# The end of the output projection in a streaming-encoder layer: another order, and four subtractions on GpSimd

## The reference, cut to what matters

```python
mix = jnp.concatenate([y_a, y_b], -1) @ w_out
x = layer_norm(ALPHA * x + (1 + g1) * mix, ln1_g, ln1_b)
h = layer_norm(x) * (1 + sc2) + sh2
gate, up = jnp.split(h @ w_ffn_up, 2, axis=-1)      # D_FF = 2816, so 22 column blocks of 128 each
ffn = (jax.nn.silu(gate) * up) @ w_ffn_down
x = layer_norm(ALPHA * x + (1 + g2) * ffn, ln2_g, ln2_b)
```

## Time and profile before

| what | value |
|---|---|
| three runs | 1384.96, 1387.47, 1394.6 us; median 1387.47 |
| the profiled execution | 1386.77 us; its span, first to last instruction, 1384.7 us |
| mean granted TensorE clock | 0.987 of full speed |
| PE, DVE, ACT, POOL busy | 96%, 68%, 42%, 40% of the span |
| output projection | about 547 to 661 us of the span |
| first pair of column blocks | about 662 to 693 us |

### The profile page before, as it was taken

The page is one execution under the profiler, slowest core; times in us unless marked ns, Lnnn a source line. Parts: engine busy times, 40 slices in busy tenths (PEclk is TensorE's granted clock), DMA queues, the critical chain, the costliest instruction groups (busy, mean ns, idle before and its releaser), DMA issues.

```text
span 1384.7 us, 28725 instructions
## 1 busy us (share of the span) xinstructions
PE 1331.2 (96%) x10596; PEld 1212.7 (88%) x10596; DVE 946.9 (68%) x1477; ACT 578.1 (42%) x1278; POOL 550.5 (40%) x622
## 2 busy tenths in 40 slices
PE   6999899989999999999899999999999999999997
PEld 4799899988977888887899999999999997887675
DVE  6526786865368877787796766556666558676388
ACT  6523343346476766244633333333333326443120
POOL 4887868682033334132234234434234331000041
PEclk9899999999999999999999999999999999999999
DMA  9422344345356653522314543545534459995894
GB/s 343 134 83 70 107 110 116 108 113 148 95 171 203 200 192 139 163 91 77 92 48 154 193 136 126 181 138 185 187 130 134 162 182 388 372 312 213 286 324 172
DMA packets 184404, 234.60 MB, mean 169 GB/s; under 512 B 17708, under 2 KB 118640, under 8 KB 184304
## 3 DMA queue, kind: packets, MB, share of 16 engines
q1 hardware_dynamic: 180128, 221.36, 49.1%
q10 hardware_dynamic: 4176, 11.89, 2.2%
HBM read 170.29 MB, written 61.73 MB: 168 GB/s over the span
## 4 chain that ended last, share of the span: by engine, by line
PE 56%; DVE 10%; issue 3%; ACT 3%; DMA 2%; POOL 1%; POOLq 0%; ACTq 0%; SPq 0%; DVEq 0%
PE bank L2533 30%; PE bank L2447 11%; PE bank L308 3%; PE bank L1803 2%; PE bank L2464 1%; PE bank L1840 1%; ACT hp L1909 1%; PE bank L1180 1%; DVE Lc L1632 1%; PE bank L1195 1%; DVE stat L1942 1%; DVE xt L1979 1%; DVE split L2576 1%; PE bank L1237 1%; PE bank L1226 1%
## 5 line engine op out<-in xcount | busy, mean ns | idle before, releaser
L2447 PE MATMUL bank<-split 128*128 128x512 f32 x924 | 212.4, 390 | 3.7 <-DVE split L2580 3.3
L2447 PEld LDWEIGHTS bank<-split 128*128 128x128 f32 x924 | 172.7, 188 | 45.5 <-DVE split L2576 6.8
L2533 PE MATMUL bank<-Tlo,rh 128*128 128x272 f32 x640 | 184.7, 289 | 0.0
L2533 PE MATMUL bank<-Thi,rh 128*128 128x272 f32 x640 | 184.2, 288 | 0.0
L2533 PE MATMUL bank<-Thi,rl 128*128 128x272 f32 x640 | 184.0, 288 | 0.0
L308 PE MATMUL bank<-hT_hi,whi 128*128 128x384 f32 (+1 forms) x504 | 167.8, 333 | 3.8 <-DVE wlo L298 3.6
L308 PE MATMUL bank<-hT_lo,whi 128*128 128x384 f32 (+1 forms) x504 | 165.8, 329 | 0.0
L308 PE MATMUL bank<-hT_hi,wlo 128*128 128x384 f32 (+1 forms) x504 | 165.7, 329 | 0.0
L2533 PE MATMUL bank<-hT_lo,rh 128*128 128x272 f32 x480 | 138.5, 289 | 0.0
L2533 PE MATMUL bank<-hT_hi,rl 128*128 128x272 f32 x480 | 138.4, 288 | 0.0
L2533 PE MATMUL bank<-hT_hi,rh 128*128 128x272 f32 x480 | 137.9, 287 | 0.0
(11 more groups left out here) (463 smaller groups left out, 3246.7 us busy)
## 6 DMA issues: line engine op xcount, KB each, us to landing
wada<-w_ada SPq DMA_DIRECT2D x12, 2048.0 KB, 11.0
raw<-w_up SPq DMA_DIRECT2D x40, 512.0 KB, 5.1
wsum<-w_down SPq DMA_DIRECT2D x11, 1024.0 KB, 5.6
wt<-wsum SPq DMA_DIRECT2D x11, 1024.0 KB, 4.0
rW<-wt SPq DMA_DIRECT2D x44, 256.0 KB, 6.4
split<-split SPq DMA_DIRECT2D x22, 512.0 KB, 4.9
wraw<-w_in SPq DMA_DIRECT2D x21, 512.0 KB, 4.1
rows<-convrow ACTq DMA_DIRECT2D x16, 577.5 KB, 3.7
```

What stands on the lines that cost most here:

```text
L2447: last = pe.matmul(ps[down_bank(q, r)][:], a[:, rows], w, start=(k == 0 and m == 0), stop=(k == KH - 1 and m == 2))
L2533: last = pe.matmul(ps[banks[c]][:, 0:NC], w[:, ks], a, start=(n < 3 and k == 0 and p == 0), stop=(k == 3 and p == 2), skip_group_check=True)
```

## The change

Nothing is computed differently; instructions change their engine or their place in a queue, all in steps 6 to 8.

- `ffn_lo(0, 0)` and `ffn_lo(0, 1)` (the low parts of the weights) and `split_h2(5)` and `split_h2(6)` go from VectorE to GpSimd, into steps 6 and 7, two in each.
- ScalarE's `ffn_hi(0, 0)` goes from step 7 to step 6, `modulate(5)` from step 7 to step 6, ahead of norm(6); `modulate(6)` from step 8 to step 7, ahead of norm(7); `modulate(7)` from before norm(8) to behind it.
- TensorE makes (0, 0) chunk 1 before `transposes(7)`, not after.

The diff, without the lines of `ffn_lo` for the second pair, which only wait for one more count that is always reached:

```diff
-        def ffn_lo(dve, i, j):
+        def ffn_lo(eng, i, j):
             if i == 0:
-                split_lo(dve, slot_of(j), R_FF + j + 1)
+                slot = slot_of(j)
+                eng.wait_ge(on["w_hi"], count(R_FF + j + 1))
+                eng.tensor_tensor(wlo[:, slot, :], wraw[:, slot, :], whi[:, slot, :].bitcast(F32), ALU.subtract).then_inc(on["w_lo"], 1)
                 return
...
             ffn_block(pe, 0, 0, (0,))
+            ffn_block(pe, 0, 0, (1,))
             transposes(PTILES - 1, (PTILES - 1) % 2)
-            ffn_block(pe, 0, 0, (1,))
             ffn_block(pe, 0, 1, (0,))
             transposes(PTILES, PTILES % 2)
...
# ScalarE, step(t, s)
-                if not (isinstance(t, int) and t < 2):
+                if not (isinstance(t, int) and (t < 2 or t > PTILES - 2)):
                     modulate(t - 2)
+                if isinstance(t, int) and t == PTILES - 2:
+                    act.wait_ge(on["wo_mm"], since("wo_mm", PTILES))
+                    ffn_hi(act, 0, 0)
+                    modulate(PTILES - 3)
                 if isinstance(t, int) and t == PTILES - 1:
-                    for j in range(2):
-                        act.wait_ge(on["wo_mm"], since("wo_mm", PTILES + j))
-                        ffn_hi(act, 0, j)
-                if isinstance(t, int) and t == PTILES:
-                    modulate(PTILES - 1)
+                    act.wait_ge(on["wo_mm"], since("wo_mm", TILES))
+                    ffn_hi(act, 0, 1)
+                    modulate(PTILES - 2)
...
             wo_steps(act, step)
+            modulate(PTILES - 1)
             modulate(PTILES)
...
# VectorE, step(t, s)
-                if isinstance(t, int) and t == PTILES:
-                    ffn_lo(dve, 0, 1)
...
-                if not (isinstance(t, int) and t < 2):
-                    split_h2(t - 2)
+                if not (isinstance(t, int) and (t < 2 or t > PTILES - 2)):
+                    split_h2(dve, t - 2)
...
-                if isinstance(t, int) and t == PTILES - 1:
-                    ffn_lo(dve, 0, 0)
...
# GpSimd, step(t, s)
                 pool.tensor_tensor(rstd[0:n, 0, 0:1], rstd[0:n, 0, 0:1], mhalf[0:n, 0:1], ALU.pow).then_inc(on["o_rs"], 1)
+                if isinstance(t, int) and t in (PTILES - 2, PTILES - 1):
+                    ffn_lo(pool, 0, t - (PTILES - 2))
                 pool.wait_ge(on["o_mv"], alone(pool, since("o_mv", t * 2 + 2)))
                 pool.wait_ge(on["o_n2"], alone(pool, since("o_n2", t)))
                 rstd_steps(pool, g, n, 1, LN_EPS, on["o_rs"])
+                if isinstance(t, int) and t in (PTILES - 2, PTILES - 1):
+                    split_h2(pool, t - 1)
```

More of the change, by code:

```diff
@@ L1814, in ffn_hi @@
             act.activation(whi1[:, j, :], wraw1[:, j, :], ACT.Copy).then_inc(on["w_hi"], 1)
-        def ffn_lo(dve, i, j):
+        def ffn_lo(eng, i, j):
             if i == 0:
-                split_lo(dve, slot_of(j), R_FF + j + 1)
+                slot = slot_of(j)
+                eng.wait_ge(on["w_hi"], count(R_FF + j + 1))
+                eng.tensor_tensor(wlo[:, slot, :], wraw[:, slot, :], whi[:, slot, :].bitcast(F32), ALU.subtract).then_inc(on["w_lo"], 1)
                 return
-            dve.wait_ge(on["w_hi"], R_FF + 3 + j)
-            dve.tensor_tensor(wlo1[:, j, :], wraw1[:, j, :], whi1[:, j, :].bitcast(F32), ALU.subtract).then_inc(on["w_lo"], 1)
+            eng.wait_ge(on["w_hi"], R_FF + 3 + j)
+            eng.wait_ge(on["w_lo"], R_FF + 2 + j)
+            eng.tensor_tensor(wlo1[:, j, :], wraw1[:, j, :], whi1[:, j, :].bitcast(F32), ALU.subtract).then_inc(on["w_lo"], 1)
         FIRST_BANKS = (6, 7)
@@ L1934, in wo_act, with split_h2 @@
             wo_steps(act, step)
+            modulate(PTILES - 1)
             modulate(PTILES)
+        def split_h2(eng, u):
+            n = tile_rows(u)
+            eng.wait_ge(on["h2_hi"], since("h2_hi", u + 1))
+            eng.tensor_tensor(hT_lo[:, :, tile_cols(u)], hp2[:, :, 0:n], hT_hi[:, :, tile_cols(u)].bitcast(F32), ALU.subtract).then_inc(on["h2_lo"], 1)
         def wo_dve(dve, mix):
@@ L1944, in stats @@
                 dve.bn_aggr(stat[0:n, slot, 12:14], stat[0:n, slot, 0:12]).then_inc(name, 1)
[L1946 to L1949, removed]
             def step(t, s):
@@ L1982, in step @@
                 stats(xt[0:n, s, :], n, 1, t * 4 + 4, on["o_mv"])
-                if isinstance(t, int) and t == PTILES - 1:
-                    ffn_lo(dve, 0, 0)
             wo_steps(dve, step)
-            split_h2(PTILES - 1)
-            split_h2(PTILES)
+            split_h2(dve, PTILES - 1)
+            split_h2(dve, PTILES)
         def rstd_steps(pool, g, n, slot, eps, name):
```

## The result

The changed kernel takes 1391.15 us (median of 20 runs, 1388.0 to 1396.05) against 1388.53 for the kernel before (20 runs, 1384.73 to 1394.6). The ratio is 1.0026 with a 95% interval of 1.0016 to 1.0035: slower by 3.6 us, at least 2.2 and at most 4.9. (The ratio is not that of the two medians, which lie 2.6 us apart.) The profiled execution has a span of 1387.9 us, 3.2 more than before.

A forecast was written before the change was run, and what follows sets the result against it. The prediction took the chain from norm(8) over the next weights' load and splits to (1, 0) as the bound, with TensorE close beside it. (1, 0) going from 693.86 to 695.55 adds 1.7 to 1387.47: 1389.2 us, range 1383.7 to 1394.

The forecast's parts named there:

- the 5.2 us of TensorE's time: Ahead of and in (0, 0)'s first products: 3.6 us wait plus 1.6 low clock; no gain unless norm(8) comes earlier.
- the band of +0.5 to +2.8: Change in us counted as the forecast case itself, around +1.7; chance 0.45.
- a stretch of 3.5 on x1(7): Sign of being wrong: VectorE's x1(7) taking 3.5 us would mean +3.8 instead of +1.7.
- the slower rival: At x1(7), GpSimd's ffn_lo(0, 1) gets the shared port first; (1, 0) moves +3.8, giving 1391.3 us; chance 0.22.
- Step 1: Step 6 of the kernel: GpSimd's ffn_lo(0, 0) goes ahead of VectorE's x1(6), which comes 2.4 us later.
- Step 2: VectorE's xt(7) comes at 658.1, then xg(7) waits for GpSimd's split_h2(5) and runs 661.7 to 663.0.
- Step 3: Port contest at x1(7): VectorE assumed ahead of GpSimd's ffn_lo(0, 1), x1(7) starting at 663.45, +1.3; called weakest.
- Steps 4 and 5: VectorE's chain from x1(7) to x1(8), without both ffn_lo, comes 0.35 us earlier; norm(8) ends at 678.55.
- Steps 6 and 7: ScalarE's modulate(7), queued behind norm(8), holds transposes(8) back to 681.5; TensorE is idle 5.7 us.
- step 9: Other way to (1, 0), by split_h2(7), modulate(8) and the new weights' copy: +1.7, reaching 695.55 against TensorE's 695.25.
- Step 8: TensorE from transposes(8) to (1, 0): 12.15 us plus 1.6 for the clock falling after idleness, reaching 695.25.
- the rule of the text: (1, 0), the start of the next products, moves by the end of norm(8) less 676.85.

The follow-up runs named there:

- n_full: n_order with the next weights loaded and split early, VectorE's two subtractions for them right behind the last statistics; 1387.53 us, ratio 0.9997.
- a_turn: Changed kernel with one more wait: GpSimd's ffn_lo(0, 1) waits until x1(7) is done; 1390.12 us, ratio 1.0011.
- b_mod7: Kernel before with one edit: modulate(7) moved behind norm(8) on ScalarE; 1389.62 us, ratio 1.0009.
- a_mod7: Changed kernel with modulate(7) put back ahead of norm(8) on ScalarE; 1388.87 us, ratio 1.0011.
- a_turn2: Changed kernel with both of GpSimd's ffn_lo made to wait for x1 of their step; 1387.38 us, ratio 0.9993.
- n_full2: n_full with VectorE's two subtractions for the next weights moved behind split_h2(7); 1382.31 us, ratio 0.9972.
- a_vec: Changed kernel's order with all four subtractions back on VectorE at their old places; 1389.46 us, ratio 1.0013.
- n_order: Kernel before with the change's ScalarE and TensorE order except modulate(7); on VectorE, x1 and statistics precede split_h2 in steps 6, 7; 1385.03 us, ratio 0.9978.

## Why the prediction was right, and where it was off

The side was right, and so was the main mechanism: no gain from the 5.2 us of TensorE's time, a new wait ahead of transposes(8), and slower. The size was not: the forecast of +1.7 is under the interval of +2.2 to +4.9, and +3.38 in the stretch is outside the band of +0.5 to +2.8. One of the signs of being wrong that the prediction names came up, a stretch of 3.5 on x1(7) (3.41): what happened is the slower rival, given 0.22. That the time, 1391.15, is in the range says little, since the range, 10 us wide, held every rival. That it lies next to that rival's 1391.3 is in part luck: the kernel before came out at 1388.53 and not at the 1387.47 that the forecasts start from, and from there the forecast would be 1390.2 and the rival 1392.3. By the steps:

- **Step 1** (first contest to GpSimd, +2.4): x1(6) took 3.43 instead of 1.28, 2.15 more. Right. GpSimd, issued 0.14 before x1(6), went first once split_h2(4) was done. The rule that this rests on, that a waiting GpSimd instruction goes ahead of VectorE's next one, is not general: in n_full GpSimd's tiny instruction, waiting since 674.37, stayed behind both of VectorE's subtractions.
- **Step 2** (xg(7) delayed): 1.68 instead of 1.28, where 2.0 was forecast; starting at 659.08 + 1.69 = 660.77, forecast 661.0. Right, a little oversized.
- **Step 3** failed, the one called the weakest. x1(7) was ready at 661.53 + 1.69 = 663.22 (forecast 663.45), but GpSimd's subtraction had been issued 0.07 before and took the port: 3.41. The slower rival is this mechanism, with its own price of +3.8 against the measured +3.38. a_turn shows it by taking the turn away: norm(8) 1.86 earlier. The reason given for x1(7) first, that GpSimd has a wait to pass as well, didn't hold it back.
- **Steps 4 and 5**: with step 3 as in the rival, norm(8) ends at 678.43 + 1.69 = 680.12; the rival said 680.65, the forecast 678.55. The forecast's -0.35 for VectorE's chain came out as +1.2.
- **Steps 6 and 7** (modulate(7) behind norm(8), transposes(8) held back): right, with 6.88 us for the forecast 5.7, by the lateness of step 3. b_mod7 shows that this order alone costs 1.95 of the stretch, 2.05 expected; there TensorE waits only 0.49 for transposes(8), and the loss comes by the way of step 9.
- **Step 8** (1.6 for the clock): from transposes(8) to the end of the parts it was 12.15 before and 695.55 - 0.58 - 681.34 = 13.63 now, 1.5 more. Right here; a_mod7, a_turn and a_turn2, where (1, 0) follows without a wait, lost 2.6 to 2.8 against the 11.96 of n_full2, after shorter waits.
- **Step 9** (the other way is 0.3 later): (1, 0) waited 0.58 for VectorE. Right. By the rule of the text, the end of norm(8) less 676.85, the shift is 680.12 - 676.85 = 3.27, against 3.38 measured. The rule is one for this order of ScalarE only: in a_turn it gives +1.4 and the stretch has +2.1, as there TensorE is the later one.

With parts of the change alone the stretch moved by +1.4 (a_vec, the order only), +1.95 (b_mod7, modulate(7) only) and +0.6 (a_turn2, all of it, with the contests over x1 settled). The parts don't add up to the whole by simple sums: either TensorE or the way of step 9 comes later at (1, 0), and TensorE's clock cost differs between the runs (1.5 to 2.8).

What stays open: the time of a_turn2 (ratio 0.9993) lies 1.6 us under what its stretch says; its interval reaches to within 0.1 of it.

## What to carry to other kernels

Before work is moved to the idle engine, look at who has the port at that moment and who would wait behind it: a 2.4 us subtraction that is issued 0.07 us too early cost the critical engine 2.1 us here, and one semaphore wait that lets the critical instruction go first gave 1.86 of it back. In an in-order queue, put nothing that is ready behind something that waits; here 3 us of ready ScalarE work stood behind an 8 us wait and passed it on to TensorE. And find the instruction whose end moves the next stage (norm(8) here), but keep an eye on the second way beside it: a_turn2 and n_order end norm(8) within 0.1 of each other, and their stretches are 44.96 and 41.04. An order that filled VectorE's own 2.4 us pause, with ScalarE's and TensorE's order of the change but for modulate(7), did what four moved subtractions did not.

## What the runs showed of the hardware that was not expected

A GpSimd instruction of one element per partition was held up by VectorE's two-tensor instructions like a large one: 2.21 us instead of 0.21 in n_full, and 2.28 in n_order (rstd1(8), issued at 667.84, behind VectorE's L298 and xg(8), which end at 670.04). The kernel before has it too: 1.08 at 665.07, beside VectorE's L298 of 664.90. Who has the next turn is not always the same. In the kernel before, rstd1(8) was issued at 670.14, 0.15 behind L298, and was done at 671.23, ahead of the end of xg(8), which VectorE had begun at 671.07; in n_order it was issued 0.16 behind L298 and waited for xg(8) too. No run shows what decides it. VectorE's statistics and its reads of banks did not hold GpSimd up, nor the reverse: in a_turn the subtraction beside them took 2.40, close to the 2.37 of the earlier trace rows.

What a wait cost TensorE beyond itself did not grow with its length. After waits of 1.13 (n_order, n_full2) nothing was lost; after 2.44 (a_vec), 3.31 (n_full), 3.64 (before) and 6.88 (changed) about 1.5 us; after 4.06, 4.89 and 5.30 (a_turn2, a_mod7, a_turn) 2.6 to 2.8 us. The granted clock tells the same by how long it stays at 1.2 GHz, in the windows behind the wait. n_full, where it begins high and falls only after work has begun:

```profile
679.90:681.00 1.10, 1.10 (x9) 0.98 (x10) 0.00 (x0) 0.14 (x1) 0.00 (x0) 0.66 0.05 15
681.00:682.50 1.50, 1.50 (x6) 1.50 (x6) 0.00 (x0) 1.50 (x6) 0.00 (x0) 0.50 0.87 247
682.50:684.00 1.50, 1.50 (x7) 1.50 (x6) 0.00 (x0) 1.46 (x4) 0.00 (x0) 0.61 1.15 330
684.00:686.00 2.00, 2.00 (x14) 2.00 (x13) 1.84 (x2) 1.98 (x3) 0.00 (x0) 1.00 0.37 91
```

And a_turn, where it is low from the start and for twice as long:

```profile
682.80:684.00 1.20, 1.20 (x9) 1.08 (x10) 0.29 (x1) 0.88 (x1) 0.00 (x0) 0.50 1.17 334
684.00:686.00 2.00, 2.00 (x7) 2.00 (x8) 0.94 (x1) 1.03 (x4) 0.00 (x0) 0.50 1.19 288
686.00:688.00 2.00, 2.00 (x8) 2.00 (x7) 0.00 (x0) 1.97 (x6) 0.00 (x0) 0.50 1.22 291
688.00:690.00 2.00, 2.00 (x10) 2.00 (x10) 1.60 (x2) 2.00 (x3) 0.00 (x0) 0.72 0.23 52
```

The longest wait is no exception to this. In a_turn the wait itself is still at 0.96 (677.40 to 682.70); in the changed kernel it is at 0.76 (674.50 to 681.30), so the clock falls well inside it, where TensorE has nothing to slow down. Over wait and work together, by the shares of the windows, the changed kernel is low about as long as a_turn, but only the part behind the wait costs time. What decides between the short stretch of n_full and the long one of a_turn no run here shows.
